# Rounding and subtracting two pairs of weights with one operation each, on a ring of four pairs

## The reference

```
for i in range(DEPTH):                       # mixers: da, sw, ml, da
    hn = rmsnorm(x, norm_g[i])
    if kind == 0:   y = diff_attention(hn, da_w_in[j], da_w_out[j], da_lambda[j], da_subln_g[j], ...)
    elif kind == 1: y = sliding_window_attention(hn, sw_w_in[j], sw_w_out[j], sw_sinks[j], ...)
    else:           y = mlstm(hn, ml_w_in[j], ml_b_gates[j], ml_w_out[j], ml_norm_g[j])
    x = x + y
return rmsnorm(x, final_g)
```

## Time and profile before

| | before |
|---|---|
| median of 3 runs | 1767.29 us (1766.95 to 1768.35) |
| profiled execution | 1767.73 us, of which the span 1766.0 us |
| PE busy | 1753.5 us (99%), granted clock 0.999 |
| DVE busy | 1122.9 us (64%), of which w_lo 709.6 |
| ACT busy | 904.6 us (51%), of which w_hi 614.7 |
| DMA | 313.16 MB, mean 177 GB/s |

### The profile page before, as it was taken

One profiled execution on the slowest core, in us unless ns is written; L12 is line 12 of the kernel. 1 busy time (PEld: TensorE's weight loads), 2 busy tenths in 40 slices (PEclk: granted clock), 3 DMA queues, 4 the chain that ended last, 5 costly groups with the idle time before them and its releaser, 6 DMA issues.

```text
span 1766.0 us, 24849 instructions
## 1 busy us (share of the span) xinstructions
PE 1753.5 (99%) x8268; PEld 1463.3 (83%) x8268; DVE 1122.9 (64%) x1819; ACT 904.6 (51%) x1403; POOL 38.0 (2%) x99
## 2 busy tenths in 40 slices
PE   8999999999999999999999999999999999999998
PEld 7888888888888888888888888888888888888887
DVE  6666666665658888855646455655666666666655
ACT  7454545444546666755544444444544545454543
POOL 1000000000000000000000000000000000000000
PEclk9999999999999999999999999999999999999999
DMA  8565565655565554556997699866565656556564
GB/s 244 181 188 173 174 189 157 183 173 190 180 190 162 161 144 141 167 177 169 159 166 200 191 156 181 212 175 190 179 188 158 183 176 181 176 177 182 164 214 144
DMA packets 170996, 313.16 MB, mean 177 GB/s; under 512 B 10822, under 2 KB 27788, under 8 KB 170796
## 3 DMA queue, kind: packets, MB, share of 16 engines
q1 hardware_dynamic: 170496, 311.02, 62.8%
q10 hardware_dynamic: 380, 1.08, 0.2%
q0 software_dynamic: 48, 0.13, 0.1%
HBM read 310.10 MB, written 2.10 MB: 177 GB/s over the span
## 4 chain that ended last, share of the span: by engine, by line
PE 99%; DMA 0%; issue 0%; DVE 0%; ACT 0%; SPq 0%; POOLq 0%; POOL 0%; DVEq 0%
PE acc L919 30%; PE acc L921 30%; PE acc L920 30%; PE tp L886 4%; PE sc L952 1%; PE sc L919 0%; PE sc L951 0%; PE sc L920 0%; PE sc L921 0%; DMA xres<-in_x_dram 0%; PE sc L1005 0%; PE sc L1006 0%; PE sc L988 0%; PE sc L987 0%; PE sc L1004 0%
## 5 line engine op out<-in xcount | busy, mean ns | idle before, releaser
L1700 DVE TENSOR_TENSOR w_lo<-raw,w_hi 128x1024 fp32r<-128x1024 f32 x584 | 709.6, 1223 | 489.2 <-ACT w_hi L858 488.2
L858 ACT ACTIVATE w_hi<-raw 128x1024 fp32r<-128x1024 f32 x584 | 614.7, 1058 | 489.9 <-PE acc L921 442.7
L919 PE MATMUL acc<-w_hi,xt_hi 128*128 128x512 f32 x1824 | 727.8, 399 | 0.0
L921 PE MATMUL acc<-w_hi,xt_lo 128*128 128x512 f32 x1824 | 713.0, 391 | 0.0
L920 PE MATMUL acc<-w_lo,xt_hi 128*128 128x512 f32 x1824 | 711.5, 390 | 0.0
L921 PEld LDWEIGHTS acc<-w_hi,xt_lo 128*128 128x128 f32 x1824 | 342.9, 188 | 73.3
L920 PEld LDWEIGHTS acc<-w_lo,xt_hi 128*128 128x128 f32 x1824 | 343.6, 188 | 67.2
L919 PEld LDWEIGHTS acc<-w_hi,xt_hi 128*128 128x128 f32 x1824 | 343.3, 188 | 66.7
L919 PE MATMUL acc<-w_hi,ot_hi 128*128 128x512 f32 (+1 forms) x520 | 202.8, 390 | 0.0
L921 PE MATMUL acc<-w_hi,ot_lo 128*128 128x512 f32 (+1 forms) x520 | 201.1, 387 | 0.0
L920 PE MATMUL acc<-w_lo,ot_hi 128*128 128x512 f32 (+1 forms) x520 | 200.8, 386 | 0.0
(11 more groups left out here) (269 smaller groups left out, 1085.8 us busy)
## 6 DMA issues: line engine op xcount, KB each, us to landing
raw<-in_da_w_in_dram SPq DMA_DIRECT2D x256, 512.0 KB, 3.8
raw<-in_ml_w_in_dram SPq DMA_DIRECT2D x96, 512.0 KB, 5.3
raw<-in_sw_w_in_dram SPq DMA_DIRECT2D x72, 512.0 KB, 3.8
raw<-in_da_w_out_dram SPq DMA_DIRECT2D x64, 512.0 KB, 4.3
raw<-in_sw_w_out_dram SPq DMA_DIRECT2D x32, 512.0 KB, 3.7
raw<-in_ml_w_in_dram SPq DMA_DIRECT2D x64, 256.0 KB, 5.1
raw<-in_ml_w_out_dram SPq DMA_DIRECT2D x32, 512.0 KB, 4.6
xres<-in_x_dram SPq DMA_DIRECT2D x3, 512.0 KB, 9.8
```

The source lines that it names most:

```text
L858: act.activation(w_hi[:, q:q + 2, :], raw[:, q:q + 2, :], ACT.Copy).then_inc(hi_ready, 1)
L919: pe.matmul(out_ap, k_hi, m_hi, start=start, stop=False)
L921: return pe.matmul(out_ap, k_lo, m_hi, start=False, stop=stop)
L1700: dve.tensor_tensor(w_lo[:, q:q + 2, :], raw[:, q:q + 2, :], w_hi[:, q:q + 2, :].bitcast(F32), ALU.subtract).then_inc(lo_ready, 1)
```

## The change

ACT rounds and DVE subtracts pairs p and p + 1 (p even) with one operation of 2048 numbers per partition, at the place of pair p; at the place of pair p + 1 there is none. The single operation waits for both loads and for PE to be done with pair p - 3, and raises `hi_ready` or `lo_ready` by two. The ring still has four pairs. The first job of the kernel (eight pairs) stays as it was. The text of PE and SP is the same. Side work stays where it was in the code, at odd and even numbers.

```diff
-                act.wait_ge(raw_full[p % LAG], 32 * J + 16 * (p // LAG + 1))
-                if w.kind == "ml" and w.phase == "iter" and j == 0:
-                    act.wait_ge(raw_half[p % LAG], i * 32 + 16 * (p // LAG + 1))
-                if not (j0 == 0 and w.first and p < LAG):
-                    act.wait_ge(pairs_done, PAIRS * J + p + 1 - LAG)
+                first_job = j0 == 0 and w.phase == "iter" and w.first
+                n = 1 if first_job else 2 - 2 * (p % 2)
+                for p2 in range(p, p + n):
+                    act.wait_ge(raw_full[p2 % LAG], 32 * J + 16 * (p2 // LAG + 1))
+                    if w.kind == "ml" and w.phase == "iter" and j == 0:
+                        act.wait_ge(raw_half[p2 % LAG], i * 32 + 16 * (p2 // LAG + 1))
+                if n and not (j0 == 0 and w.first and p < LAG):
+                    act.wait_ge(pairs_done, PAIRS * J + p + n - LAG)
                 q = 2 * (p % LAG)
-                act.activation(w_hi[:, q:q + 2, :], raw[:, q:q + 2, :], ACT.Copy).then_inc(hi_ready, 1)
+                if n:
+                    act.activation(w_hi[:, q:q + 2 * n, :], raw[:, q:q + 2 * n, :], ACT.Copy).then_inc(hi_ready, n)
...
-                dve.wait_ge(hi_ready, PAIRS * J + p + 1)
+                first_job = j0 == 0 and w.phase == "iter" and w.first
+                n = 1 if first_job else 2 - 2 * (p % 2)
                 q = 2 * (p % LAG)
-                dve.tensor_tensor(w_lo[:, q:q + 2, :], raw[:, q:q + 2, :], w_hi[:, q:q + 2, :].bitcast(F32),
-                                  ALU.subtract).then_inc(lo_ready, 1)
+                if n:
+                    dve.wait_ge(hi_ready, PAIRS * J + p + n)
+                    dve.tensor_tensor(w_lo[:, q:q + 2 * n, :], raw[:, q:q + 2 * n, :], w_hi[:, q:q + 2 * n, :].bitcast(F32),
+                                      ALU.subtract).then_inc(lo_ready, n)
```

## The result

The changed kernel takes 1916.90 us (1915.21 to 1920.71, 4 runs) against 1767.24 (1766.95 to 1768.35): ratio 1.0853, interval 1.084 to 1.0866, 150 us slower. The sign and the kind of loss were forecast, its size was not: 98 us, with a range that ended at 1910. The profiled execution took 1920.7 us with a span of 1919.0, 153.0 more than before.

A forecast was written before the change was run, and what follows sets the result against it. The prediction took TensorE to bound the kernel from end to end, so only its waits count. Stalls of 49 + 12 + 28 + 7 + 2 = 98 us on the profiled 1767.7 gave 1866 us, range 1830 to 1910.

The forecast's parts named there:

- The operations' cost, the order and the date: Operations of 2048 take 1.91 us (ScalarE) and 2.28 (VectorE); pairs ready 4.4 to 4.5 later, odd side work behind them.
- Sliding-window layer: Four iterations: waits for the key product, score bank and p_lo copies, 12.3 us each, 49 us in all.
- Differential attention: Eight iterations: rotary embedding and gated output come late, 1.5 us each, 12 us in all.
- The three links: Differential attention, each iteration: gated output loses 0.7 us, rotated query and rotated key 0.4 each.
- mLSTM: mLSTM layer: gates, weights that arrive late, and gate and mix elsewhere, 28 us; least certain term, 10 to 45.
- Late loads: mLSTM layer: refill starts later where DMA engines have no time to spare; two stalls of 8 us, 16 in all.
- Gates: First mLSTM iteration: three small VectorE links with TensorE waiting lose 2.4, 3.5 and 3.9 us, together 9.8.
- Output products: Output jobs of four layers: residuals and second transposes come late, 2.2 us in three layers, 0.7 in the last: 7.
- A: Rival: the stalls as summed in the prediction, 1866 us, own range 1840 to 1892; chance 0.68.
- B: Rival: the later refill of loads binds everywhere, 1965 us at the worst, 1910 if only half; chance 0.14.
- C: Rival: half the stalls, as some cover each other or operations are nearer their lower bounds, 1815 to 1840 us; chance 0.15.
- D: Rival: not slower, the scheduler's distances hold and only the end's 2 us is lost, 1769 us; chance 0.03.

The follow-up runs named there:

- The idle matmuls: Changed kernel with twelve idle 128x128 matmuls on PE before the waits of scores 0 and 2 in the sliding-window layer: 1903.06 us, ratio 1.0777.
- the late date alone: Kernel before the change, single operations at their own places, but an even pair's rounding waits for pair p - 3: 1797.71 us, ratio 1.0174.

## Why the prediction was wrong in size

**The step that failed** is the price of a wait. The prediction took each wait at its own length and gave TensorE's clock nothing. The two traces differ by 153 us, 55 more than the 98. An estimate from the pair steps puts some 26 of the 55 to matmuls at the lower clock level: 19 in the sliding-window layer, 4.4 at the gates, and 1.5 each in the middle mLSTM iteration and in the last output jobs. The other 29 are waits that were taken too short or not seen, 8 of them in the sliding-window layer.

**The operations' cost, the order and the date**: right. 1.91 and 2.28 were taken, 1.92 and 2.29 measured; both pairs are ready 4.6 after end(2g-3) (median), where 4.4 to 4.5 was written, since ScalarE starts 0.26 after it and not 0.20, and VectorE 0.10 after ScalarE and not 0.04. The date decides the sum, and the saving in busy time counted for nothing, so the rule cited from the Trainium skill ("VectorE: DVE Perf Modes", section "The TRN2 errata") holds for the engines' busy time (48 and 36 us less) and says nothing of the kernel's.

**Sliding-window layer, 49 against 76.5.** This is where that step cost most. Each wait was nearly right. In the second iteration with the clock restored: score 0 3.4 (predicted 3.5), score 2 3.7 (3.2), score 4 2.2 (2.1), score 6 1.5 (1.3), and the probabilities and outputs 3.6 over four pairs (2.2). That makes about 57 for four iterations. The term that was missing is TensorE's clock: a wait was priced at its length, and the matmuls behind it at 0.227 us. The idle matmuls take back 14 us of it by the medians, 16 between the two traces; the other 3 are the two stretches at the lower level that are left there. The granted clock was 1.00 in the rows of before, where PE never waits; the prediction took it for given. The Trainium skill ("TensorE: Matmul & The Clock Gate", section "HAM oscillation — how this bites in real kernels") describes waits between blocks of matmuls after which each block starts cold again; the trace agrees, with VectorE in the place of its DMA: behind the wait of 3.32 us the matmuls start 0.42 us apart.

**Differential attention, 12 against 19 (17.8 inside the iterations).** The three links were named rightly and lost 0.88, 0.80 and 0.72 against 0.7, 0.4 and 0.4. The error is small and systematic: the start of the rounding after end(k), 0.26, was left out in the link of `gs`, and the hand-over from ACT to DVE was taken as 0.04 where 0.10 is measured. Some 0.2 to 0.4 us on each of 24 stalls makes nearly all of the 7 us.

**mLSTM, 28 against 40.7.** Late loads: 16 predicted, 16.5 measured, but that the totals agree is luck. The two stalls of 8 were placed at pair 3 behind two stretches of full DMA use; those steps lost 1.8 and 1.6, of which 1.0 is the gated output. The rest came as a dozen stalls of 0.3 to 2.3, most of them in the middle iteration. Gates: the links before the products of 4, 7 and the turn of 12 lost 2.7, 1.9 and 4.3 (2.4, 3.5, 3.9), and then half clock behind two of them, 4.4. One link was not seen, the entry of the layer, 4.9 at pair 2:

```profile
914.40 2.29 DVE L1707 TENSOR_TENSOR w_lo<-raw,w_hi 128x2048 fp32r<-128x2048 f32 x1 [3.15 <-ACT w_hi L862]
916.61 1.28 DVE L1689 TENSOR_TENSOR xres<-xres,acc 128x512 f32<-128x512 f32 x2
921.32 2.29 DVE L1707 TENSOR_TENSOR w_lo<-raw,w_hi 128x2048 fp32r<-128x2048 f32 x1 [3.43 <-ACT w_hi L862]
923.52 1.66 DVE L1275 SCALAR_TENSOR_TENSOR xt_lo<-tp,gcol,xt_hi 128x256 fp32r<-128x256 f32 x4
```

The last residual (3) and the last split of x (5) are both odd, one behind each of two double operations, and the gates' product needs that split.

**Output products, 7 against 14 (15.3 by the edges).** 2.8 to 3.2 in each of the first three layers (2.2), since each link lost some 0.1 to 0.2 more than written, and 5.1 in the last (0.7), where 4.2 come at pairs 15 and 16: ACT waits 5.7 us for a load there, with slow matmuls behind. SP issues the 1 MB of `final_g` between the loads of pairs 16 and 17, and the double rounding needs both. That it is the cause was not tried.

**Rivals.** A had the mechanism and 1866, but its own range ended at 1892. B (loads bind everywhere) falls with the late date alone, 1797.7, and holds only in the mLSTM layer, where it had its own term. C erred in the wrong direction: no stall of the sum was covered by another, and the operations did not come near the lower bounds. D is out: score 2 waits 3.4 us in every iteration. Nothing among the rivals made a wait cost more than its length, and the range ended below the result.

## What to carry to other kernels

Merging two operations on this ring cost twice: all that is written behind them was late by the second one, and a producer and a consumer that had overlapped piece by piece ran one after the other. That second part, 83 us of 150, was the larger. Merge only where the bound engine has two pieces in hand and nothing behind the merged operation is wanted early. When a forecast adds waits of some 3 us to a TensorE that never waited, price them at more than their length: here about 57 us of waits in the sliding-window layer brought some 19 us of matmuls at half clock with them.

## What was not expected of the hardware

- TensorE fell to 1.2 GHz after waits of 3.32 and 3.40 us: 512-column matmuls started 0.427 us apart for about 2.6 us or more, then 0.227 again. With idle matmuls in the wait the granted clock of the layer was 0.99 in place of 0.92. The length of the wait alone does not decide it: after the change it fell behind several waits of 1.94 to 2.64 us too, but stayed at 1.00 behind one of 3.42 us (799 to 806 us).
- The DMA engines' busy share says little of what they move: with loads in two transfers of 256 KB (first mLSTM job of the second iteration) it was 0.92 at 143 GB/s (1034 to 1047 us), in the rest of that iteration 0.64 at 183 GB/s, and from 1145 to 1223 us 0.94 at 161 GB/s. It does not go by the form of the loads: from 1119 to 1145 us, with the same two transfers for most pairs, it was 0.68 at 181. What makes the difference was not found.
